# Top-4 choice by value replacement in a hybrid layer with 32 experts, and other edits around the start of the expert stage

## The reference, cut to what matters

```
hn     = rmsnorm(h)                                   # 256 x 1024
logits = hn @ w_router + b_router                     # 256 x 32
top_vals, top_idx = top_k(logits, 4); top_w = softmax(top_vals)
gates  = top_w at top_idx, 0 elsewhere                # 256 x 32
for e in range(32):
    g, u = split(hn @ w_gu[e] + b_gu[e])              # 1024 + 1024
    act  = (clip(u, -7, 7) + 1) * min(g, 7) * sigmoid(1.702 * min(g, 7))
    out += gates[:, e] * (act @ w_down[e] + b_down[e])
result = rmsnorm(h + out)
```

## Time and profile before

| | us |
|---|---|
| median of 3 runs | 1071.06 |
| lowest and highest | 1070.61, 1073.69 |
| the profiled execution, whole | 1072.88 |
| its span, first to last instruction | 1071.1 |
| TensorE products, share of the span | 93% |
| weight loads of TensorE | 39% |
| VectorE (DVE) | 22% |
| ScalarE (ACT) | 13% |
| GpSimd (POOL) | 1% |
| HBM read | 419.56 MB |

### The profile page before, as it was taken

How to read it: one execution, slowest core, us unless ns; L and a number is a source line. 1 busy time by engine, 2 the same in 40 slices (tenths; PEclk the granted TensorE clock), 3 DMA queues, 4 the chain that set the end, 5 groups by cost and what they waited for, 6 DMA issues and landing times.

```text
span 1071.1 us, 12922 instructions
## 1 busy us (share of the span) xinstructions
PE 1000.1 (93%) x5798; PEld 414.1 (39%) x5799; DVE 240.3 (22%) x533; ACT 137.2 (13%) x262; POOL 15.8 (1%) x26
## 2 busy tenths in 40 slices
PE   8989979999999999999999999998999999899996
PEld 6865444333333333333333333323333333333332
DVE  2996341111111111111111111101111111110112
ACT  4125221101010101000101010000101000000002
POOL 3000020000000000000000000000000000000000
PEclk9999989999999999999999999999999999999999
DMA  9983349999999999999999999999999999999993
GB/s 317 409 353 133 139 155 411 428 428 428 427 427 427 428 426 429 426 428 429 426 427 428 428 427 428 427 428 427 430 427 425 428 428 428 427 427 427 428 427 146
DMA packets 39097, 421.49 MB, mean 393 GB/s; under 512 B 5137, under 2 KB 9281, under 8 KB 14464
## 3 DMA queue, kind: packets, MB, share of 16 engines
q1 hardware_dynamic: 37232, 420.31, 93.6%
q10 hardware_dynamic: 1808, 0.33, 0.2%
HBM read 419.56 MB, written 1.05 MB: 393 GB/s over the span
## 4 chain that ended last, share of the span: by engine, by line
PE 55%; DMA 35%; DVE 6%; ACT 2%; issue 1%; SPq 0%; DVEq 0%; ACTq 0%
PE work L939 48%; DMA ring<-in_w_gu 35%; PE resid L939 5%; DVE main L870 2%; DVE main L867 2%; DVE main L863 2%; PE work L1247 1%; ACT main L572 1%; DMA ring<-in_w_dw 1%; PE work L1054 0%; PE work L1136 0%; DVE top_i L806 0%; DVE main L932 0%; SPq L292 0%; ACT work L418 0%
## 5 line engine op out<-in xcount | busy, mean ns | idle before, releaser
L939 PE MATMUL work<-ring,main 128*64 128x512 f32 (+1 forms) x3104 | 687.2, 593 | 26.7 <-DMA ring<-in_w_gu 25.0
L939 PEld LDWEIGHTS work<-ring,main 128*64 128x64 f32 (+1 forms) x3104 | 223.1, 138 | 478.7 <-issue 425.5
L863 DVE TENSOR_SCALAR main<-work 128x512 f32<-128x512 f32 x32 | 22.1, 692 | 753.6 <-PE work L939 753.6
L572 ACT ACTIVATE main<-main 128x512 f32<-128x512 f32 x32 | 20.2, 631 | 503.3 <-DVE main L863 503.3
L939 PE MATMUL work<-ring 128*128 128x256 f32 (+1 forms) x288 | 72.1, 412 | 0.0
L939 PE MATMUL resid<-main 128*128 128x512 f32 x136 | 71.2, 612 | 0.9 <-DVE main L923 0.9
L583 ACT ACTIVATE main<-work 64x512 f32<-64x512 f32 x63 | 37.3, 592 | 227.6 <-PE work L939 227.3
L939 PE MATMUL work<-bgu_rows,ident 128*64 128x512 f32 x256 | 61.6, 602 | 0.0
L939 PEld LDWEIGHTS work<-ring 128*128 128x128 f32 x288 | 55.6, 194 | 15.0 <-issue 8.2
L939 PEld LDWEIGHTS work<-select,main 128*128 128x128 bf16 x1584 | 49.1, 99 | 26.9 <-issue 26.9
L939 PE MATMUL work<-select,main 128*128 128x64 bf16 x1584 | 53.1, 195 | 0.9 <-DVE select L848 0.9
(11 more groups left out here) (174 smaller groups left out, 250.3 us busy)
## 6 DMA issues: line engine op xcount, KB each, us to landing
ring<-in_w_gu SPq DMA_DIRECT2D x128, 2048.0 KB, 41.7
ring<-in_w_down SPq DMA_DIRECT2D x64, 2048.0 KB, 41.7
ring<-in_w_in SPq DMA_DIRECT2D x3, 2048.0 KB, 14.9
ring<-in_w_in SPq DMA_DIRECT2D x4, 1024.0 KB, 12.1
ring<-in_w_out SPq DMA_DIRECT2D x2, 2048.0 KB, 19.5
main<-in_x SPq DMA_DIRECT2D x2, 512.0 KB, 4.3
result<-main SPq DMA_DIRECT2D x4, 256.0 KB, 2.5
ring<-in_norm_final_g SPq DMA_DIRECT2D x1, 512.0 KB, 16.2
```

Of the source, the lines that this page charges most:

```text
L572: nc.scalar.activation(sig_h, gate_h, ACT.Sigmoid, scale=SWIGLU_ALPHA).then_inc(sig_ready, 1)
L863: V.tensor_scalar(gate_h, work[:, GATE_BANK, :], SWIGLU_LIMIT, None, ALU.min).then_inc(gate_clamped, 1)
L939: return nc.tensor.matmul(out_, lhsT, rhs, start=start, stop=stop, skip_group_check=True)
```

## The change

1. `choose()` no longer finds indices. The four lower of the eight maxima are overwritten by a sentinel 3e38, and so are four extra columns behind the 32 logits. MATCH_REPLACE puts -3e38 where a logit equals one of the eight values. An expert is chosen where the result differs from the logit. The weights are formed over all 32 experts, masked by `chosen`.
2. The router product is turned over: the hidden state is stationary, the weights (32 columns) stream, and the logits come out with tokens on partitions. ScalarE's copies and the transposes back are gone.
3. The bf16 parts of block 1 are made in two halves of 512 columns; its third part is now DVE's, one half ahead of `choose()`, one behind `chosen_b`. GpSimd makes only block 0's third part, ahead of its memset.
4. While DVE chooses, TensorE runs two products on the identity (`keep_warm`) and expert 0's biases.
5. `add_bdown` moves from expert 0 to expert 2.
6. Chunk number 11 is loaded in two halves: the first as soon as the first row block of expert 0 has been used.
7. `copy_h_turned(1, 1)` stands ahead of the reciprocal of block 1's norm.

```diff
     def uses_of(e, i):
-        return (CHUNKS * e + i) // SLOTS + 1
+        number = CHUNKS * e + i
+        return number // SLOTS + 1 + int(number >= SLOTS and number % SLOTS == 0)
...
+            def load_first_reused(e, i):
+                f = 4 * P * (i - UP_CHUNKS)
+                src = w_down[e, f:f + 4 * P, :].rearrange("(p b) n -> p b n", b=4)
+                for half, (used, count_) in enumerate(((first_unit_used, 1), (slots_used, 1))):
+                    sp.wait_ge(used, count_)
+                    to = unit(half).rearrange("p (b n) -> p b n", b=2)
+                    sp.dma_start(to, src[:, 2 * half:2 * half + 2, :]).then_inc(slot_full[0], 16)
...
+                    if number == SLOTS:
+                        load_first_reused(e, i)
+                        continue
...
+            nc.gpsimd.memset(logits[:, :, E:E + 8 - TOP_K], SENTINEL).then_inc(sentinels_ready, 1)
...
+            pool.wait_ge(part_act, 2)
+            nc.gpsimd.tensor_tensor(hn_parts[0][2], hn[0], hn_parts[0][1], ALU.subtract).then_inc(part_pool, 1)
             pool.wait_ge(h_done, 3)
             nc.gpsimd.memset(bdown_sb, 0.0).then_inc(moe_zeroed, 1)
-            third_part(0)
-            pool.wait_ge(logits_turned, TB)
+            pool.wait_ge(logits_done, TB)
             nc.gpsimd.memset(gates_t, 0.0).then_inc(moe_zeroed, 1)
-            third_part(1)
...
-            cast_part(1, 0)
+            cast_first_part(1, halves[0])
+            cast_first_part(1, halves[1])
+            cast_second_part(1, halves[0], 2)
+            cast_second_part(1, halves[1], 3)
             act.wait_ge(moe_zeroed, 1)
             act.dma_start(bdown_sb[0:E, :], b_down).then_inc(bdown_in, 16)
-            copy_logits(0)
-            copy_logits(1)
-            cast_part(1, 1)
...
-            dve.wait_ge(count_ready, 2)
-            then(V.tensor_scalar(expert_no[:, :], count[:, 0:E], -1.0, None, ALU.add))
...
             def choose():
                 for t in range(TB):
-                    dve.wait_ge(logits_turned, t + 1)
-                    V.scalar_tensor_tensor(logits[:, t, :], work[:, CHOICE_BANKS[t], 0:E], stat[:, 14 + t:15 + t], br_row[:, :],
+                    dve.wait_ge(logits_done, t + 1)
+                    V.scalar_tensor_tensor(logits[:, t, 0:E], work[:, LOGITS_BANKS[t], 0:E], stat[:, 14 + t:15 + t], br_row[:, :],
                                            ALU.mult, ALU.add).then_inc(logits_scaled, 1)
                 for t in range(TB):
                     dve.wait_ge(logits_scaled, t + 1)
-                    V.max(out=top8[:, t, :], in_=logits[:, t, :]).then_inc(largest_ready, 1)
+                    V.max(out=top8[:, t, :], in_=logits[:, t, 0:E]).then_inc(largest_ready, 1)
+                dve.wait_ge(largest_ready, TB)
+                V.memset(top8[:, :, TOP_K:8], SENTINEL).then_inc(lowest_masked, 1)
+                dve.wait_ge(lowest_masked, 1)
+                dve.wait_ge(sentinels_ready, 1)
                 for t in range(TB):
-                    dve.wait_ge(largest_ready, t + 1)
-                    done = V.max_index(out=top8_i[:, t, :], in_max=top8[:, t, :], in_values=logits[:, t, :])
-                then(done)
-                then(V.tensor_copy(top_i[:, :, :], top8_i[:, :, 0:TOP_K]))
-                for t in range(TB):
-                    V.tensor_tensor(onehot[:, 0, t, :, :], ..., ALU.is_equal).then_inc(onehot_ready, 1)
-                for t in range(TB):
-                    V.tensor_reduce(chosen[:, t, :], ..., AX.X, ALU.add).then_inc(choice_ready, 1)
-                V.tensor_copy(chosen_b[:, :, :], chosen[:, :, :]).then_inc(chosen_ready, 1)
+                    V.match_replace(out=others[:, t, :], in_to_replace=top8[:, t, :], in_values=logits[:, t, :], imm_value=-SENTINEL)\
+                        .then_inc(others_ready, 1)
+                dve.wait_ge(others_ready, TB)
+                V.tensor_tensor(chosen_b[:, :, :], others[:, :, 0:E], logits[:, :, 0:E], ALU.not_equal).then_inc(chosen_ready, 1)
+                third_part(1, halves[1], 6)
+                V.tensor_tensor(chosen[:, :, :], others[:, :, 0:E], logits[:, :, 0:E], ALU.not_equal).then_inc(choice_ready, 1)
+                V.tensor_tensor(weights[:, :, :], logits[:, :, 0:E], top8[:, :, 0:1].to_broadcast([P, TB, E]), ALU.subtract)\
+                    .then_inc(top_diff, 1)
...
             copy_h_turned(1, 1)
-            less_first_part(1)
+            dve.wait_ge(h_root, 2)
+            V.reciprocal(stat[:, 15:16], stat[:, 13:14]).then_inc(h_scale, 1)
+            dve.wait_ge(h_scale, 2)
+            less_first_part(1, halves[0], 3)
+            less_first_part(1, halves[1], 4)
+            third_part(1, halves[0], 5)
             choose()
...
-                    last = mm(work[0:E, LOGITS_BANKS[t], 0:P], wr_sb[:, kb, :], h_t[t][:, kb, :], kb == 0, kb == KB - 1)
+                    last = mm(work[:, LOGITS_BANKS[t], 0:E], h_t[t][:, kb, :], wr_sb[:, kb, :], kb == 0, kb == KB - 1)
...
-            turn_logits(1)
+            pe.wait_ge(bgu_in, 16)
+            keep_warm(2, work[:, GATE_BANK, 0:P])
+            bias(0)
...
                     if kb % 2 == 1:
                         last.then_inc(slots_used, 1)
+                    elif is_first and kb == 0:
+                        last.then_inc(first_unit_used, 1)
...
-                bias(e)
+                if e > 0:
+                    bias(e)
...
-                if e == 0:
+                if e == 2:
                     add_bdown()
```

More of the change, by code:

```diff
@@ L167, in hybrid_layer @@
         count = sb("count", [P, SEQ], F32)
-        expert_no = sb("expert_no", [P, E], F32)
         cols = sb("cols", [P, 36], F32)
@@ L178, in hybrid_layer @@
         asum = sb("asum", [P, len(GROUPS), 4], F32)
-        logits = sb("logits", [P, TB, E], F32)
+        logits = sb("logits", [P, TB, E + 8 - TOP_K], F32)
+        others = sb("others", [P, TB, E + 8 - TOP_K], F32)
         top8 = sb("top8", [P, TB, 8], F32)
-        top8_i = sb("top8_i", [P, TB, 8], U32)
-        top_i = sb("top_i", [P, TB, TOP_K], F32)
-        top_w = sb("top_w", [P, 3, TB, TOP_K], F32)
+        weights = sb("weights", [P, TB, E], F32)
         top_s = sb("top_s", [P, 2, TB], F32)
@@ L532, in square_h1, with cast_first_part, cast_second_part @@
                             h_squared)
-            def cast_part(t, n):
-                if n == 0:
-                    act.wait_ge(h_scale, t + 1)
-                    nc.scalar.activation(hn_parts[t][0], hn[t], ACT.Copy, scale=stat[:, 14 + t:15 + t]).then_inc(part_act, 1)
-                else:
-                    act.wait_ge(part_dve, t + 1)
-                    nc.scalar.activation(hn_parts[t][1], hn[t], ACT.Copy).then_inc(part_act, 1)
-            def copy_logits(t):
-                act.wait_ge(logits_done, t + 1)
-                nc.scalar.activation(logits_t[:, t * P:(t + 1) * P], work[0:E, LOGITS_BANKS[t], 0:P], ACT.Copy)\
-                    .then_inc(logits_t_ready, 1)
+            def cast_first_part(t, cut):
+                act.wait_ge(h_scale, t + 1)
+                nc.scalar.activation(hn_parts[t][0][:, cut], hn[t][:, cut], ACT.Copy, scale=stat[:, 14 + t:15 + t]).then_inc(part_act, 1)
+            def cast_second_part(t, cut, rests):
+                act.wait_ge(part_dve, rests)
+                nc.scalar.activation(hn_parts[t][1][:, cut], hn[t][:, cut], ACT.Copy).then_inc(part_act, 1)
+            whole, halves = slice(0, D), (slice(0, HALF), slice(HALF, D))
             act.wait_ge(h_copied, 1)
@@ L551, in _ @@
             root_h(0)
-            cast_part(0, 0)
-            cast_part(0, 1)
+            cast_first_part(0, whole)
+            cast_second_part(0, whole, 1)
             square_h1(0)
@@ L556, in _ @@
             root_h(1)
-            cast_part(1, 0)
+            cast_first_part(1, halves[0])
+            cast_first_part(1, halves[1])
+            cast_second_part(1, halves[0], 2)
+            cast_second_part(1, halves[1], 3)
             act.wait_ge(moe_zeroed, 1)
             act.dma_start(bdown_sb[0:E, :], b_down).then_inc(bdown_in, 16)
-            copy_logits(0)
-            copy_logits(1)
-            cast_part(1, 1)
             act.wait_ge(top_diff, 1)
-            nc.scalar.activation(top_w[:, 1, :, :], top_w[:, 0, :, :], ACT.Exp).then_inc(top_exp, 1)
+            nc.scalar.activation(weights[:, :, :], weights[:, :, :], ACT.Exp).then_inc(top_exp, 1)
             act.wait_ge(gates_turned, 1)
@@ L828, in _ @@
             inv_rms(0, stat[:, 8:9], (stat[:, 10:11], stat[:, 12:13]), stat[:, 14:15], h_squared, h_mean, h_root, h_scale)
-            less_first_part(0)
+            less_first_part(0, whole, 1)
             for half in (slice(0, HALF), slice(HALF, D)):
@@ L1165, in _, with bias @@
             route(1, range(0, KB // 2))
-            turn_logits(0)
             pe.wait_ge(ht_ready, 4)
             route(1, range(KB // 2, KB)).then_inc(logits_done, 1)
-            turn_logits(1)
+            def bias(e):
```

(12 more changed lines are left out.)

66 lines of the change are left out of this document (27 added, 39 removed).

## The result

Five executions of the changed kernel have a median of **1067.17 us** (1065.82 to 1068.75); five of the kernel before on the same chip, in turn with them, 1073.69 (1070.61 to 1074.63). The ratio is 0.995, with a 95% interval of 0.9937 to 0.9964: 3.9 to 6.8 us less. The forecast was 1064.3 in a range of 1062.3 to 1067.8, and faster by over 0.3%. The sign and the range hold; the number is 2.9 too low. The profiled execution of the changed kernel is its fastest, 1065.82, with a span of 1064.1.

What follows compares the result with a forecast made beforehand. The weight stream's lasting start, set by chunk 15's issue, was taken as the bound. up(0) 5.24 earlier, b_down 1.53 and the split brought it 6.8 earlier; span 1071.1 became 1064.3, the predicted median, range 1062.3 to 1067.8 us.

Steps and rivals of the forecast that it cites:

- 6.8 earlier, 0.0 after that. The tail is unchanged: Weight stream runs for good from 172.7, not 179.5 us; nothing more gained or lost from there to the end.
- Bound by the start of the stream: Whole kernel: the end is set by when the weight stream starts for good, plus fixed bytes and a fixed tail.
- B: Rival: TensorE, not the stream, sets the end, so b_down's cost in expert 2 counts; 1067.0 us, chance 0.05.
- Router turned over: Router products: 0.12 us each, the last 24 ending at 141.7, 0.2 us ahead of before.
- The choice: DVE's expert choice: two value replacements at 0.41 us together; chosen_b at 143.97, 2.70 earlier; place 2.12 earlier.
- C: Rival: MATCH_REPLACE is dear, the choice comes late and the clock falls; 1072.3 us, slower than before, chance 0.03.
- Held by GpSimd: In the choice, GpSimd's 2.12 us third part held DVE's cast to 1.99; the new order leaves only a short memset.
- The clock: Without TensorE's long idle before the places, full clock: gather 1.57 us instead of 2.72, biases 1.92 instead of 3.03.
- rival A: The clock falls all the same, at gather; 1066.9 us, chance 0.17.
- b_down moved: From expert 0 to 2: chunk 15's slot another 1.53 us earlier; 2.64 of TensorE in expert 2, hidden by the stream.
- The split: Chunk 11 in two halves: first half issued 1.82 us earlier, but worth only 0.5, not 1.8.
- Chunk 15 sets the stream: Chunk 15's issue counts, not chunk 11's: issued at 170.98 instead of 177.75 us, with a hole of 0.9 ahead.

Runs made afterwards that it cites:

- after_again: The changed kernel, unedited, run again in later rounds; 1066.66 us against 1072.68 for the kernel before.
- bdown_first: Changed kernel with add_bdown back in expert 0; 1068.11 us.
- before_warm: Kernel before the change, plus sixteen identity products on TensorE while DVE chooses; 1070.32 us against 1072.85 for the kernel before.
- late_choice2: Changed kernel with six more half-block subtractions on DVE ahead of choose(); 1074.32 us, ratio 1.0012 to the kernel before.
- no_bdown: Changed kernel without b_down's eight products in expert 2, waits kept, output biases missing from the result; 1068.62 us.
- third_on_pool: Changed kernel with block 1's third part made on GpSimd in halves instead of on DVE; 1068.00 us.
- bias_behind: Changed kernel without keep_warm and with expert 0's biases back behind its gather; 1070.02 us.
- warm_gap: Changed kernel with six identity products on TensorE in expert 0's gap; 1066.97 us.
- warm_both: Changed kernel with six identity products in expert 0's gap and fourteen in the wait for the convolution's taps; 1065.54 us.
- best2: warm_both with chunk 15 loaded in halves too, against the changed kernel; 1065.30 us, and 1065.12 us when repeated.

## Why the prediction was right, and where it failed

*What failed first is the last step of the sum, its base:* "the median of three runs, 1071.06, happens to equal the span. Predicted median: 1064.3." The sum was made in the profiled execution, 1072.88 with a span of 1071.1, and 6.8 taken from that gives 1066.1; taken from the low median of three it gives 1064.3. The 1.8 between span and execution are there after the change too (1065.82 and 1064.1), and the kernel before has a median of 1072.7 to 1073.7 in all later rounds. By the profiled execution the forecast is 1066.1, against 1066.66 to 1067.17 as medians. The prediction named both numbers and chose the one that fits no step of its own working. Of the 2.9 us of error, 1.8 are this.

*What failed second is "6.8 earlier, 0.0 after that. The tail is unchanged",* a term put at nothing. In after_again the lead is 6.4 at 1030 us, 4.6 at the last wait for weights and 3.7 at the end: 2.7 lost. Over the thirteen profiles the loss from 1030 us on is 0.0 to 2.7. The prediction took the stream for one queue with one end, where a chunk counts when the slowest of its sixteen parts is in. In the change's first profile the term does hold (7.1 at 1030 us, 7.1 at the last wait, 7.0 in the span). How much of the remaining 1.1 us of error this loss holds, and how much the clock in expert 0 (below), stays open, since one execution of a kernel was profiled and not the median one.

*Luck.* The span, 1064.1 for a forecast 1064.3, is in part luck: this execution is the fastest of its five, and 0.57 of its gain arose ahead of the change. That the median is inside the range is luck too, as the range was laid around a number 1.8 too low. Its lower end is also 0.3 below its own three bounds: 0.3 + 0.5 + 0.9 taken from 1064.3 gives 1062.6.

*The gain.* Forecast 6.8; 7.0 between the two profiles, of which 0.57 arose ahead of the change; 6.5 between the medians, 5.4 by the ratio of the rounds, 6.0 on repetition. So it came out somewhat small, not large.

*Bound by the start of the stream:* right up to 1030 us. The lead at 1030 us is that at 200 us within 0.3 in all profiles but bdown_first (0.7), and before_warm and late_choice2 move it by what they move `up`. B falls: no_bdown gives TensorE about 2.4 us in expert 2 (gather to turn_act is 5.78 after, 3.38 there) and nothing at the end.

*Router turned over:* right, 0.115 each for 0.12. The 24 weight loads fill the same 2.76 us as the products. By the Trainium skill (TensorE: Matmul & The Clock Gate, LDWEIGHTS) a load of 128 columns takes 107 ns; the trace agrees within 8 ns.

*The choice:* right in kind. A MATCH_REPLACE8 takes 0.18 and its load of values 0.09, as its sister; `chosen_b` comes 0.2 before the forecast time when the 0.57 is added back, and `place` 0.5 before it, as DVE's three operations between the two take 0.78 together and not 1.07. C's mechanism exists (late_choice2), its price doesn't. No run takes the new choice, the router or the halves out by themselves, so their shares rest on these rows.

*Held by GpSimd:* right, and third_on_pool sharpens it: there the comparison with two operands in SBUF is held (1.18), while MATCH_REPLACE8 is not (0.18). The Trainium skill (SBUF — State Buffer, SBUF: two separate sides) has such a two-operand operation wait for a GpSimd one; the trace agrees.

*The clock:* the size was right (2.25 in before_warm, 1.15 + 1.11 reckoned), the reason only half. "Without the long idle I expect full clock": bias_behind has 2.65 idle and half clock. The products and biases in the gap, which the prediction counted only as time out of the way, are what holds it. And rival A was looked for at one place, the gather. Seven profiles have neither b_down nor a filler in expert 0's gap; in six of them, after_again among them, the clock falls behind it, between 164 and 175.

*b_down moved:* right by the trace (20.84 and not 22.33 from first issue to chunk 15), and free in expert 2 as forecast, with 429 GB/s there. Not foreseen: its products kept TensorE at work right up to turn_act; without them it idles 1.82 there, ahead of the 0.73 behind turn_act. Where the clock falls on that, as in after_again, 1.49 of the term's 1.53 is given back: the prediction had put the clock's price there at nothing.

*The split:* right that it is worth far less than 1.8. *Chunk 15 sets the stream:* right, hole 0.9 forecast and 0.9 measured in the change's first profile.

## What to carry to other kernels

Make the sum and the forecast in the same execution: if the sum rests on a profile, the base is that profile's own time, not a median of a few runs taken elsewhere. Work that is moved out of a gap on TensorE has two prices, its time and the clock behind the gap; look at every later gap of that kind, not only at the one that is filled. Where a stream has to restart, look for the last chunk that it has to wait for, since an earlier issue of the first one is hidden behind it. A lead of the stream as a whole isn't yet a lead at the end: look also at when the last part of the last load lands.

## What the runs showed of the hardware

- TensorE's granted clock fell to 0.50, 1.2 GHz, within an idle gap of 2.65 us (from 139.75 on; the fall is at 141.2), with the router's products of 32 columns ahead of it (bias_behind). In late_choice2 a gap of 4.62 us ended at 146.94 and the clock fell at 147.7. Behind the changed kernel's 1.82 and 0.73 in expert 0 it fell in one profile and not in another of the same program.
- When a gap is filled, the fall can come at the next one: at 194 to 198 in expert 1 in bdown_first and warm_gap, where the same program unfilled had stayed at 1.00. It need not: before, warm_both and both profiles of best2 are filled too and stay at 1.00 there.
- The low clock ends at varying times. From 78 us on it was 0.50; in 82 to 84 us it reads 0.50 before and 0.63 after, and in 84 to 86 us 0.85 and 1.00, at the same place of the program. That is 0.56 us of TensorE time, and the work behind it starts 0.57 us earlier.
- A DVE comparison of 64 elements took 0.23 where it began as GpSimd went from one operation to the next, and 1.18 right behind that, while MATCH_REPLACE8 kept its 0.18 beside the same GpSimd work.
- The first byte of a reissued chunk came 1.4 us after the issue in the changed kernel (149.12 to 150.52) and 1.7 in the kernel before.
- The sixteen parts of a 2 MiB load landed over 1.2 us at 146 us and over 8.8 us at 1045 us in the kernel before, with 427 GB/s in between; in the other kernels the last spread is 8.8 to 10.7 us. Whoever waits for a whole load waits for the slowest part.
